# Three transformer blocks on one core: MLA's rotary key with its weights held still, modulation sums and last bias moved into the borders, and unread products of the identity in TensorE's waits

## The reference, cut to what matters

```
block 1: x = LN(a*x + even_mixer(x));  x = LN(a*x + swiglu(x))        # gated linear attention + RWKV-7
block 2: x = LN(a*x + mla(x));         x = LN(a*x + swiglu(x))        # latent attention
block 3: mod = silu(c) @ w_ada + b_ada; sh1, sc1, g1, sh2, sc2, g2 = split(mod, 6)
         x = x + g1 * rms(mixer(rms(x) * (1 + sc1) + sh1))
         x = x + g2 * rms(relu(h @ w1 + b1)**2 @ w2 + b2)             # h = rms(x) * (1 + sc2) + sh2
mla:     p = x @ w_in;  cq, ckv, k_pe = p[:768], p[768:1024], p[1024:1056]
         q = rms(cq) @ w_q_b;  kv = rms(ckv) @ w_kv_b;  k_pe = rope(k_pe)      # k_pe shared by 16 heads
```

## Time and profile before

| | us |
|---|---|
| median of 3 runs | 1177.11 |
| lowest and highest | 1174.06 and 1177.56 |
| the profiled execution | 1179.13 |
| its span | 1177.3 |
| busy: PE, DVE, ACT, POOL | 1098.4, 725.2, 517.8, 135.9 |

### The profile page before, as it was taken

How to read it: one execution, slowest core, us unless ns; L and a number is a source line. 1 busy time by engine, 2 the same in 40 slices (tenths; PEclk the granted TensorE clock), 3 DMA queues, 4 the chain that set the end, 5 groups by cost and what they waited for, 6 DMA issues and landing times.

```text
span 1177.3 us, 16940 instructions
## 1 busy us (share of the span) xinstructions
PE 1098.4 (93%) x7036; PEld 970.4 (82%) x7036; DVE 725.2 (62%) x1005; ACT 517.8 (44%) x737; POOL 135.9 (12%) x151
## 2 busy tenths in 40 slices
PE   7989899988999999879889899999789997999998
PEld 7878898867999988667667899998578877999885
DVE  4576864576675665846674676675655557666343
ACT  4452342254443433425663454443365656655331
POOL 1005852114000000600001300000200000000000
PEclk9898999888999999879999899999979999999999
DMA  9430002143987686235772687777433332665540
GB/s 303 153 113 31 1 1 73 72 143 122 311 273 237 223 308 244 76 141 172 102 221 72 218 284 261 240 261 282 136 128 126 105 108 76 197 193 182 198 157 36
DMA packets 113598, 193.67 MB, mean 165 GB/s; under 512 B 4691, under 2 KB 85090, under 8 KB 113395
## 3 DMA queue, kind: packets, MB, share of 16 engines
q1 hardware_dynamic: 109986, 180.18, 45.7%
q0 software_dynamic: 3248, 11.83, 4.6%
q10 hardware_dynamic: 288, 0.59, 0.1%
HBM read 188.39 MB, written 4.19 MB: 164 GB/s over the span
## 4 chain that ended last, share of the span: by engine, by line
PE 83%; DVE 8%; ACT 4%; issue 2%; DMA 1%; POOL 1%; DVEq 0%; SPq 0%; ACTq 0%; POOLq 0%
PE ps L433 23%; PE ps L434 22%; PE ps L435 22%; PE ps L2011 2%; PE ps L1996 2%; PE ps L1225 2%; PE ps L1989 1%; PE ps L1235 1%; PE ps L1462 1%; PE ps L1169 1%; DVE XL L572 1%; DVE ARR L400 1%; ACT ARR L387 1%; PE ps L502 1%; DMA ring<-in_ffn_w_gate_up_dram 1%
## 5 line engine op out<-in xcount | busy, mean ns | idle before, releaser
L400 DVE TENSOR_TENSOR ARR<-ring,ARR 128x2048 fp32r<-128x2048 f32 (+3 forms) x142 | 319.0, 2251 | 210.5 <-ACT ARR L387 210.4
L433 PE MATMUL ps<-XH,ARR 128*128 128x256 f32 x1232 | 355.5, 289 | 15.1 <-DVE XL L572 8.9
L387 ACT ACTIVATE ARR<-ring 128x2048 fp32r<-128x2048 f32 (+3 forms) x142 | 265.3, 1875 | 203.4 <-PE ps L435 158.1
L434 PE MATMUL ps<-XL,ARR 128*128 128x256 f32 x1232 | 352.2, 286 | 0.0
L435 PE MATMUL ps<-XH,ARR 128*128 128x256 f32 x1232 | 351.8, 286 | 0.0
L433 PEld LDWEIGHTS ps<-XH,ARR 128*128 128x128 f32 x1232 | 238.5, 194 | 21.8 <-issue 15.9
L434 PEld LDWEIGHTS ps<-XL,ARR 128*128 128x128 f32 x1232 | 238.7, 194 | 0.3 <-issue 0.2
L435 PEld LDWEIGHTS ps<-XH,ARR 128*128 128x128 f32 x1232 | 238.5, 194 | 0.0
L433 PE MATMUL ps<-ARR 128*128 128x512 f32 x420 | 171.4, 408 | 7.8 <-DVE ARR L524 4.6
L434 PE MATMUL ps<-ARR 128*128 128x512 f32 x420 | 168.1, 400 | 0.0
L435 PE MATMUL ps<-ARR 128*128 128x512 f32 x420 | 168.0, 400 | 0.0
(11 more groups left out here) (345 smaller groups left out, 1277.8 us busy)
## 6 DMA issues: line engine op xcount, KB each, us to landing
ring<-in_ffn_w_gate_up_dram SPq DMA_DIRECT2D x44, 1024.0 KB, 6.2
ring<-in_w_dram SPq DMA_DIRECT2D x32, 1024.0 KB, 5.2
ring<-in_w_ada_dram SPq DMA_DIRECT2D x24, 1024.0 KB, 5.4
ring<-in_ffn_w_down_dram SPq DMA_DIRECT2D x22, 1024.0 KB, 5.0
ring<-in_even_w_in_dram SPq DMA_DIRECT2D x13, 1024.0 KB, 5.5
ring<-in_w_in_dram SPq DMA_DIRECT2D x9, 1024.0 KB, 5.4
ring<-in_mla_w_q_b_dram SPq DMA_DIRECT2D x6, 768.0 KB, 6.6
ring<-in_even_w_out_dram SPq DMA_DIRECT2D x4, 1024.0 KB, 4.9
```

Of the source, the lines that this page charges most:

```text
L387: e.activation(split(i)[0], raw(i), ACT.Copy).then_inc(*up("hi", ("hi", i)))
L400: e.tensor_tensor(lo, raw(i), hi.bitcast(F32), ALU.subtract).then_inc(*up("lo", ("lo", i), ("raw free", i)))
L433: e.matmul(out, lhs[0], rhs[0], start=first, stop=False)
L434: e.matmul(out, lhs[0], rhs[1], start=False, stop=False)
```

## The change

1. `mpe` is computed with its weights stationary (32 columns) and the 256 tokens streaming: 24 products instead of 48, by `pe_rope_key`. Its result is a 32 x 256 column block, copied by ACT (`KPT`) and turned back by two small transposes. `min` gets `tail=2`, and half 0's norm is written ahead of half 1's, with the correction of `mqb`'s first two pieces put between and behind the halves. One reciprocal serves both sums of a half.
2. The modulation columns 1, 2 go from `down` into border `n1`, on DVE behind `dve_norm`; 4, 5 go between block 2's end and `m0`, on DVE behind `dve_scaled` of `m0`. The gate's gain is multiplied in before the sum over partitions (`dve_gate_gain`).
3. The bias `b2` (four products of one row, line 486) starts the four banks of `w2` in border `m1`, and is no longer added at the end. `w1` then turns in four banks.
4. `pe_busy` issues n products of 128 columns of the identity with itself into a bank that nobody reads: 9 (of zeros) and 10 at the start, 17 after `tob`, 10 and 8 in `n0`, 3 in `n1`, 11 after `cq`, 7 and 8 in `n2`, 15 and 7 in `m0`, 2 and 7 in `m1`.
5. At the start the halves of x are copied ahead of the split of the first weight piece, but for the last.

```diff
+        def pe_busy(e, name, n, of=None):
+
+            use = ("busy", name)
+            b = bank(e, use)
+            x = ident if of is None else of
+            for _ in range(n):
+                k = e.matmul(b[:, 0:P], x, x, start=True, stop=True)
+            k.then_inc(*up("busy", ("free", use)))
+
+        def pe_transposed(e, tag, src, c_n, ready, between=None):
             before = [banks.take((tag, c)) for c in range(c_n // 2)]
             for t in range(2):
+                if t and between:
+                    between(e)
...
         def pe_norm(e, i):
-            pe_transposed(e, f"n{i}", XN, 8, xn_ready(i))
+
+            def between(e):
+                if i == 1:
+                    pe_modulation_column(e, 1)
+                pe_busy(e, ("n", i, 0), (10, 3, 7)[i])
+
+            pe_transposed(e, f"n{i}", XN, 8, xn_ready(i), between)
+            if i == 1:
+                pe_modulation_column(e, 2)
+            else:
+                pe_busy(e, ("n", i, 1), 8)
...
+            act_halves(e, "x0", XT, 8, [], slice(0, 3))
             act_split(e, weights[0])
-            act_halves(e, "x0", XT, 8, [])
+            act_halves(e, "x0", XT, 8, [], slice(3, 4))
...
         def pe_start(e):
+            e.wait_ge(*at("zeros"))
+            pe_busy(e, "zeros", 9, GB[:, 0, 0:P])
             pe_transposed(e, "x0", X, 8, lambda t: ["x low"] if t else ["ident", "x top"])
+            pe_busy(e, "x0", 10)
...
+        def dve_gate_gain(e, j):
+
+            g, acc = G12[:, j // 3, :], ACCA[:, j % 2, :]
+            e.wait_ge(*at(("gate rows", j // 3)))
+            e.wait_ge(*now("ada"))
+            e.tensor_tensor(acc, acc, GN, ALU.mult).then_inc(*up("ada", ("gain in", j)))
+            e.tensor_tensor(g, g, GN, ALU.mult).then_inc(*up("ada"))
...
             pe_rows(e, ("down", layer), 22, 1024, HT, lambda c: ("ht", layer, 2 * c),
-                    between={6: lambda e: pe_modulation_column(e, 3 * layer + 1),
-                             20: lambda e: pe_modulation_column(e, 3 * layer + 2)}, tail=2)
+                    tail=2)
...
         def pe_mla_projections(e):
-            pe_rows(e, "min", 8, 1024, XT, xt_step("n1"))
-            pe_rows(e, "mpe", 8, 32, XT, xt_step("n1"))
+            pe_rows(e, "min", 8, 1024, XT, xt_step("n1"), tail=2)
+            pe_rope_key(e)
             pe_transposed(e, "cq", CQ, 8, lambda t: [("cq", t)])
+            pe_rope_key_rows(e)
+            pe_busy(e, "cq", 11)
             pe_rows(e, "mqb", 6, 1536, CT, xt_step("cq"))
...
+        def pe_rope_key(e):
+
+            w = place_of["mpe", 0]
+            b = bank(e, "mpe")
+            e.wait_ge(*at(("lo", w)))
+            for c in range(8):
+                k = mm3(e, b[0:32, 0:256], cut(split(w), ALL, c), cut(XT, ALL, c), c == 0, c == 7)
+            k.then_inc(*up("products", ("used", w), ("full", "mpe")))
...
+                e.wait_ge(*at(("cq root", t, 1)))
+                e.reciprocal(both, both).then_inc(*up("cq"))
+                e.wait_ge(*now("cq"))
+                for j, (c, acc, y) in enumerate(parts):
                     e.tensor_scalar(c, c, acc, None, ALU.mult).then_inc(*up("cq", *([("cq", t)] if j else [])))
+                dve_split(e, place_of["mqb", t])
             dve_scaled(e, "cq", CT, lambda c: vec(0, 95 + c), None, ("xt", ("n1", 2)))
...
+        def pe_last_bias(e):
+
+            e.wait_ge(*at("b2"))
+            for n, i in enumerate((0, 1, 6, 7)):
+                t, j = n // 2, n % 2
+                b = bank(e, ("w2", t, j), i)
+                e.matmul(b, ones1, BT2[0:1, 512 * j:512 * j + 512], start=True, stop=False)
+            banks.first, banks.n = 2, 4
...
             pe_ffn(e, 1, 3)
+            pe_modulation_column(e, 4)
+            pe_modulation_column(e, 5)
+            pe_busy(e, ("m", 0, 0), 15)
             pe_transposed(e, "m0", XN, 8, m_ready(0))
+            pe_busy(e, ("m", 0, 1), 7)
             pe_in2(e)
             pe_attend(e, SWA, pe_beside_heads)
             pe_out2_rest(e)
+            pe_last_bias(e)
+            pe_busy(e, ("m", 1, 0), 2)
             pe_transposed(e, "m1", XN, 8, m_ready(1))
+            pe_busy(e, ("m", 1, 1), 7)
             pe_w1_w2(e)
...
             dve_norm(e, 1, ("xt", ("n0", 2)))
+            dve_modulation_column(e, 1)
+            dve_modulation_column(e, 2)
             dve_mla_projections(e)
...
             dve_scaled(e, "m0", XT, mod_scale(0), mod_shift(0), ("xt", ("n2", 2)))
+            dve_modulation_column(e, 4)
+            dve_modulation_column(e, 5)
             dve_in2(e)
```

More of the change, by code:

```diff
@@ L171, in __init__ @@
     def __init__(self, aps):
-        self.aps, self.held, self.place, self.turn, self.n = aps, {}, {}, 0, 8
+        self.aps, self.held, self.place, self.turn, self.first, self.n = aps, {}, {}, 0, 0, 8
     def take(self, use):
-        i = self.turn % self.n
+        i = self.first + self.turn % self.n
         self.turn += 1
@@ L191, in second @@
     def second(self):
-        self.held, self.place, self.turn, self.n = {}, {}, 0, 8
+        self.held, self.place, self.turn, self.first, self.n = {}, {}, 0, 0, 8
 def program(nc, a):
@@ L456, in parts_of, with pe_rows @@
             return [(o, min(512, n - o)) for o in range(0, n, 512)]
-        def pe_rows(e, tag, kc, n, xT, xready, bias=None, between=None, tail=1):
+        def pe_rows(e, tag, kc, n, xT, xready, begun=False, between=None, tail=1):
             parts = parts_of(n)
@@ L463, in pe_rows @@
                 for j in range(len(parts)):
-                    before[t, j] = banks.take((tag, t, j))
+                    before[t, j] = None if begun else banks.take((tag, t, j))
             per = max(1, 2048 // n)
@@ L508, in flat_bank, with act_halves @@
             return ps(use).rearrange("p (c t) -> p c t", c=2)
-        def act_halves(e, tag, dst, c_n, before):
-            for c in range(0, c_n, 2):
+        def act_halves(e, tag, dst, c_n, before, part=slice(None)):
+            for c in range(0, c_n, 2)[part]:
                 use = (tag, c // 2)
@@ L517, in act_halves, with dve_halves @@
                 e.activation(dst[0][:, c:c + 2, :], flat_bank(use), ACT.Copy).then_inc(*up("first", ("first", use)))
-        def dve_halves(e, tag, dst, c_n):
-            for c in range(0, c_n, 2):
+        def dve_halves(e, tag, dst, c_n, part=slice(None)):
+            for c in range(0, c_n, 2)[part]:
                 use = (tag, c // 2)
@@ L1813, in pe_mla_projections, with pe_rope_key_rows @@
                 pe_rows(e, f"mkv{half}", 2, 1024, cut(CT, ALL, slice(6, 8)), lambda c: ("xt", ("cq", 3)))
+        def pe_rope_key(e):
[5 more added lines that the diff above has]
+            k.then_inc(*up("products", ("used", w), ("full", "mpe")))
+        def pe_rope_key_rows(e):
+            b = bank(e, "kp")
+            e.wait_ge(*at("kpt"))
+            for t in range(2):
+                k = e.transpose(b[:, 32 * t:32 * t + 32], KPT[:, t * P:t * P + P], ident[0:32, 0:32])
+            k.then_inc(*up("turned", ("full", "kp")))
         def act_mla_projections(e):
             for k0 in range(0, 8, 2):
-                act_split(e, ahead("min", k0, k0 < 6))
+                act_split(e, ahead("min", k0, k0 < 4))
+            act_split(e, place_of["mpe", 0])
             for t in range(2):
@@ L1827, in act_mla_projections @@
                     e.activation(acc, acc, ACT.Sqrt, bias=eps_rms, scale=1.0 / n).then_inc(*up("mla", ("cq root", t, j)))
+                act_split(e, place_of["mqb", t])
+            e.wait_ge(*at(("full", "mpe")))
+            e.activation(KPT, ps("mpe")[0:32, 0:256], ACT.Copy).then_inc(*up("mla", "kpt", ("free", "mpe")))
             act_scaled(e, "cq", CT, lambda c: vec(0, 95 + c), None, [], ("xt", ("n1", 3)))
@@ L1906, in dve_mla_projections @@
[L1906 to L1916 removed]
+                e.tensor_copy(CQ[:, t, 0:512], ps(("min", t, 0))).then_inc(*up("cq", ("free", ("min", t, 0))))
@@ L2260, in mod_shift @@
             return lambda c: MOD[:, 24 * k + c:24 * k + c + 1]
[L2262 removed]
+        mods = [("mod in", j) for j in (0, 1)]
         carve = Carve(0)
```

62 lines of the change are left out of this document (28 added, 34 removed).

## The result

The changed kernel takes 1161.44 us (median of 4 runs, 1159.79 to 1164.57) where the kernel before, in the same comparison, takes 1177.34 (1174.06 to 1182.89). The ratio is 0.9863, with a 95% interval of 0.982 to 0.9906, which is 11 to 21 us. The prediction was 1163, with a range of 1154 to 1171. The profiled execution took 1161.64, its span is 1159.8: 17.5 less than before. Comparisons further down are of the medians with their intervals where whole kernels are meant, and of landmarks in two traces (the start of the same instruction in each) where one stage is meant.

A forecast was written before the change was run, and what follows sets the result against it. TensorE, busy 93% of the span, was taken as the bound, except in borders where it waits for norms and often drops to half clock. Terms summed to 14.4 us: 1179.1 to 1164.7 by profile, 1162.7 by median, said 1163; range 1154 to 1171.

The forecast's parts named there:

- the two late pieces: Second `min` piece and third `mqb` piece would come late from DVE; TensorE waits 3.4 and some 2.8 us.
- Start, 1.0: Start: fillers give back at most 2.6 us, but the first product comes up to 0.8 later; 1.0 taken.
- `tob`, 1.9: Behind `tob`: 17 fillers fill 3.7 of 4.6 us, and the 10 products behind them run faster; 1.9 us back.
- n0 0.8 and n2 0.5: Norm borders n0 and n2: fillers in the waits give 0.8 us (at most 1.6) and 0.5 (0 to 1.1).
- Columns in `down`, 3.4 each: Modulation sums, 1.68 and 1.72 us, leave each of two `down` stages: 3.4 us each, 6.8 together.
- n1, -3.1: Border n1: column reads delay the second `min` piece 1.3 us, and a clock fall in the wait costs 1.8.
- Key, 9.3, less 1.6 for the fall: `min` to `mqb`: scaling of `cq` 9.3 us sooner; clock fall before the third `mqb` piece costs 1.6.
- m0, -4.5: Border m0: second filler row waits for column 4's bank and runs at half clock, delaying `va2`; net -4.5 us.
- Bias 4.2, m1 -0.7: Four bias products, 1.05 us each, leave `w2`: 4.2 gained; in border m1 they cost 0.7 (0 to 3).
- the second: Rival: no falls in the `min` and `mqb` waits, n0 whole, m1 free: 4.9 us more, 1158; chance 0.2.
- The third: Rival: clock falls in borders despite fillers, transposes and one-row products leaving too little: 1167, to 1170; chance 0.15.
- The fourth: Rival: unread identity products do not hold the clock, take 0.43 us each and delay the path: 1180; chance 0.05.

The follow-up runs named there:

- e5: Kernel before with only the bias change: four one-row products start `w2`'s banks in border m1; no fillers. 1173.54 us, ratio 0.9951.
- e9: e8 with unread products only at the start and after `tob`, none in later borders. 1153.62 us, ratio 0.9776.
- e10: e8 with no unread products at all, so the m0 bank edit falls away. 1158.41 us, ratio 0.9823.
- e3: Changed kernel, but DVE reads columns 1 and 2 behind the corrections of the second and third `min` pieces. 1159.78 us, ratio 0.9826.
- e2: Changed kernel, but m0's second row of fillers takes the first row's bank, which nobody reads. 1158.61 us, ratio 0.9824.
- e7: Kernel before with only the key change: stationary weights, `min` tail 2, order of the halves' norms; no fillers. 1170.19 us, ratio 0.992.
- e4: Changed kernel, but the rope's angles are computed behind `mpe`'s split instead of behind the scaling of `cq`. 1157.72 us, ratio 0.9811.
- e8: Changed kernel with the edits of e2, e3 and e4 together. 1151.65 us, ratio 0.9755.

## Why the prediction was right, step by step

By the medians 15.9 us went, by the spans 17.5; the sum had 14.4. The mechanisms foretold for the columns, the key, the two late pieces and the bank in m0 all stand in the trace. The total is closer than its parts: by the spans the terms for start and `tob`, key, m0 and bias were 5.1 us too small together, those for n0 and n2 2.0 too large, and that these partly cancel is luck. The terms:

- **Start, 1.0.** The first product comes later, as the moved copies said: at 11.9 on average in the eight kernels that have them, at 11.1 in the four that do not. From there to the last one-row product near 36 us (the earlier trace rows has it at 37.08) the six traces with fillers take 23.4 to 23.5 us. Of the six without, five take 24.9 to 26.1 (before 25.9), but e5 takes 23.4: its products were 0.12 us apart from the start, without any filler. So the fillers bring 0 to 2.6 here, and fillers and copies together put that product 2.0 sooner in this pair of traces, and 0.9 sooner if the six filled traces (35.3 on average) are held against the four of the old order (36.2). The term was sound. Up to the second half of the mixer the same groups stand at 256.2 and 259.8, so start and `tob` together are 3.6 (3.95 in the pair), where I had 2.9. The 4.8 of e9 and e10 is the fillers alone, with the copies moved in both; what start and what `tob` bring of it was not measured apart.
- **`tob`, 1.9.** Measured 1.85 in after: the stretch at 249.3 has clock 1.00.
- **n0 0.8 and n2 0.5.** Measured -0.3 and -0.4. The clock was full, as said, and the second piece was begun 8.9 us after the first instead of 10.5: the whole bound of 1.6. But the fourth and fifth pieces then came late (0.46 and 0.79 us at 300.71 and 307.43; 0.79 at 665.79 behind n2). In the chain of waits of after a transfer issued at 288.54 lasts 7.76 us, ACT's split and DVE's correction follow it, and the fourth piece begins; ahead of the fifth piece's correction DVE still does two multiplications of a modulation piece (2.6 us from 302.47). I had looked at one piece beyond the border and not at the transfers.
- **Columns in `down`, 3.4 each.** Measured 3.6 in block 1. **n1, -3.1.** Measured -3.2; the wait of 2.98 and the fall at 490 stand where they were foretold, and e3 shows that the wait comes from the reads' place. The fall is not certain with it: in e2, with the same code, it did not come, and n1 cost 1.6.
- **Key, 9.3, less 1.6 for the fall.** (The recorded sum has 7.5, 0.2 less than these two give.) Measured 9.7 and 1.7; the 1.7 is the whole stage against before, and without a fall behind its wait (e3) it was 0.1. The scaling of `cq` begins at 513.5, 6.2 us after the last `min` product; e7 shows that it is the order of DVE and ACT, e4 that the third piece hangs on the angles.
- **m0, -4.5.** Measured -3.2: in the table 4.4 less 4.0, and 3.6 of the 4.4 are `down`'s. The second row of fillers began at 847.94, 5.55 behind the transposes' end and 0.05 after DVE had read column 4 behind its last XL, at half clock (3.35 for seven, 3.0 said), and e2 shows the bank as the cause. With `down`'s share the term is +0.4 where I had -1.1.
- **Bias 4.2, m1 -0.7.** Measured 5.1 and, from `in2` on, 0.4 gained. The row was 1.05 of the chain for one product; what a product adds to the stage is 1.2 to 1.3 (5.1 us for four in after, 4.8 in e5). That term was mis-sized by reading a chain's piece for a step.

Among the rivals, of the second (no falls in the new waits, n0 whole, m1 free) only the last came in after: m1 lost nothing, but both waits brought falls. That falls are not bound to come there is seen in e2 (none before the second `min` piece) and e3 (none before the third `mqb` piece). The third's main mechanism did not come: with transposes between fillers the granted clock was 1.00 behind `tob` and in n0 and n2. The fourth needed half clock in a row of fillers; it came in m0 after 5.55 us of standing, and in part in m1, and in m0 it did cost.

Open: what makes the scan between 37 and 245 us, which the change does not touch, take anything from 206.5 to 212.0 us in the twelve traces. With fillers at the start its mean is 208.3, without them 209.9, which such a spread does not tell apart. A stretch at half clock near 36 us stands in all of them but e8, some 3 us long in after, e2, e4 and e5 and some 7 in the others, so the fillers that run before 11 us do not decide it.

## What to carry to other kernels

An unread product is not free: it takes a bank, and where the turn gives it one that a late reader holds, the filler blocks everything behind it (5 us here, more than all fillers in later borders bring). Before filling a wait, ask which piece is needed two and three steps beyond it: full clock is worth nothing if a correction or a transfer ends last, and it can cost: the wait before the late piece grows, and the clock may fall in it (the fillers after `cq`, 1.6 us). Small reads on a second engine cost nothing while the stage behind them has slack; when another edit takes that slack, as the key did, their place must be chosen anew.

## What was not expected of the hardware

The clock can fall while TensorE is busy in the records. In e5 TensorE was busy without a gap at full clock from 955 to 973.16, then four one-row products ran, and nothing else stands in that border. The clock falls at 975.2, while they run, stays at half (1.2 GHz) through the 16 transposes, and is full (2.4) when `w1` begins after a further wait of 1.60 us:

```profile
973.16 5.21 PE L2506 MATMUL ps<-GB,CST 1*128 1x512 f32 x8
978.30 3.67 PE L500 MATMUL ps<-CST,XN 128*128 128x128 f32 x16
983.58 0.36 PE L433 MATMUL ps<-XH,ARR 128*128 128x256 f32 x1 [1.60 <-DVE XL L570]
```

```profile
974.60:978.30 3.70, 3.70 (x6) 0.98 (x4) 3.26 (x9) 2.87 (x6) 0.00 (x0) 0.58 0.00 0
978.30:981.90 3.60, 3.60 (x17) 3.27 (x16) 1.28 (x3) 1.26 (x3) 0.00 (x0) 0.50 0.00 0
983.50:990.00 6.50, 5.21 (x42) 5.03 (x43) 4.70 (x6) 5.67 (x6) 0.00 (x0) 1.00 0.00 0
```

Between half and full lie transposes and a wait alone: what the earlier trace rows showed at 979.2 is repeated. The Trainium skill, page TensorE: Matmul & The Clock Gate, section PE-mode transpose, has it that transposes do not bring the full clock; this trace disagrees a second time.

A wait of the same length does not always cost the clock. Before the third `mqb` piece TensorE stood 2.54 us in after, and the next 4.4 us had 0.61; in e2 it stood 2.54 us too, and the clock was 0.50 for 2.5 us behind it; in e3, after 2.55 us at the same place, no fall followed. So the price of such a wait, 0 or up to 1.7 us, is not settled by its length, and one trace of a kernel does not give it.
